# Ten ring slots for twelve, gathers worked on two at a time, and ten weight chunks kept for both blocks

## What is computed

```python
for i in range(DEPTH):                      # DEPTH = 2
    y = rmsnorm(h, mix_norm_g[i])
    h = h + (mixer_ab(y, ...) if i == 0 else mixer_conformer(y, ...))
    y = rmsnorm(h, ffn_norm_g[i])
    h = h + peer(y, peer_w_q[i], peer_sub_keys[i], peer_u[i], peer_v[i])
return rmsnorm(h, final_norm_g)[:, 16:272]

def mixer_conformer(y, ...):
    a, g = split(y @ w_pw1 + b_pw1)         # w_pw1: 1024 x 2048
    z = causal_depthwise_conv(a * sigmoid(g), conv_w) + conv_b   # 31 taps
    return silu(layernorm(z)) @ w_pw2 + b_pw2

def peer(y, w_q, sub_keys, u, v):
    q = (y @ w_q).reshape(T, 8, 2, 128)
    # top 16 of 128 keys for each half, then the top 16 of the 256 sums
    gate = softmax(top_val)
    act = gate * gelu(sum_d(u[expert] * y))
    return sum over heads and experts of act * v[expert]
```

## Time and profile before

| | us |
|---|---|
| median of 3 runs (1606.29 to 1609.34) | 1606.82 |
| the profiled execution | 1606.77 |
| its span, first to last instruction | 1605.0 |

### The profile page before, as it was taken

How to read it: one execution, slowest core, us unless ns; L and a number is a source line. 1 busy time by engine, 2 the same in 40 slices (tenths; PEclk the granted TensorE clock), 3 DMA queues, 4 the chain that set the end, 5 groups by cost and what they waited for, 6 DMA issues and landing times.

```text
span 1605.0 us, 19986 instructions
## 1 busy us (share of the span) xinstructions
PE 1046.8 (65%) x6936; PEld 711.0 (44%) x6936; DVE 1111.9 (69%) x3119; ACT 461.3 (29%) x953; POOL 500.8 (31%) x541
## 2 busy tenths in 40 slices
PE   8997876757734577778574477877576444544454
PEld 8995642525511266656362155665263111211111
DVE  3436878676457776997756777987765777777764
ACT  4111553111111345742111335743222111111110
POOL 0003333333223333332322323332332333333330
PEclk9998877867955699888796589877788555555666
DMA  9979999999999999999999999999999999999994
GB/s 369 408 259 402 374 420 421 417 421 420 416 420 420 421 378 415 420 415 394 422 416 420 421 411 403 417 405 374 420 418 419 421 422 421 421 421 423 420 420 190
DMA packets 105300, 646.70 MB, mean 403 GB/s; under 512 B 11632, under 2 KB 15728, under 8 KB 37616
## 3 DMA queue, kind: packets, MB, share of 16 engines
q0 software_dynamic: 76032, 553.68, 83.5%
q1 hardware_dynamic: 25536, 89.66, 14.2%
q10 hardware_dynamic: 3632, 2.08, 0.4%
HBM read 644.33 MB, written 1.05 MB: 402 GB/s over the span
## 4 chain that ended last, share of the span: by engine, by line
DMA 40%; PE 28%; DVE 15%; POOL 5%; issue 5%; ACT 4%; DVEq 2%; POOLq 0%; ACTq 0%
DMA ring<-in_uv_dram,expert 36%; PE ps L691 14%; DVE ring L1221 7%; PE ps L868 7%; POOL ring L406 5%; DMA wring<-in_wall_dram 5%; PE ps L881 2%; DVE side L1276 2%; PE ps L698 1%; PE ps L909 1%; ACT side L590 1%; PE ps L856 1%; ACT yg L471 1%; ACT osb L651 1%; ACT L475 0%
## 5 line engine op out<-in xcount | busy, mean ns | idle before, releaser
L1221 DVE CUSTOM_DVE_ANT_0 ring<-ring,ps 128x1024 f32<-128x1024 f32 x528 | 634.8, 1217 | 314.9 <-DMA ring<-in_uv_dram,expert 261.2
L406 POOL DMA_INDIRECT ring<-in_uv_dram,expert x528 | 498.7, 945 | 1068.8 <-PE ps L868 808.2
L868 PE MATMUL ps<-ring,mix 128*32 128x512 f32 x2112 | 369.3, 834 | 327.3 <-DVE mix L1237 327.3
L868 PEld LDWEIGHTS ps<-ring,mix 128*32 128x32 f32 x2112 | 67.8, 135 | 531.7 <-DVE mix L1237 391.0
L665 ACT ACTIVATE gel<-dots 128x4 f32<-128x4 f32 x132 | 27.1, 205 | 761.7 <-DVE dots L1221 761.4
L691 PE MATMUL ps<-yT,wring 128*128 128x128 f32 (+1 forms) x1184 | 159.6, 294 | 48.2 <-DMA wring<-in_wall_dram 27.6
L691 PEld LDWEIGHTS ps<-yT,wring 128*128 128x128 f32 x1184 | 150.7, 202 | 63.6 <-DMA wring<-in_wall_dram 34.2
L881 PE MATMUL ps<-sel,osb 128*128 128x16 f32 x528 | 84.1, 304 | 70.6 <-ACT osb L651 70.6
L881 PEld LDWEIGHTS ps<-sel,osb 128*128 128x128 f32 x528 | 80.7, 241 | 108.9 <-ACT osb L651 108.9
L590 ACT ACTIVATE side<-ident,params 128x128 f32<-128x128 f32 x310 | 96.3, 389 | 15.6 <-PE ps L909 14.8
L856 PE MATMUL ps<-ident,yg 128*128 128x128 f32 x264 | 48.0, 342 | 58.0 <-DVE dots L1221 58.0
(11 more groups left out here) (211 smaller groups left out, 1135.5 us busy)
## 6 DMA issues: line engine op xcount, KB each, us to landing
wring<-in_wall_dram SPq DMA_DIRECT2D x102, 512.0 KB, 11.8
ring<-in_wall_dram SPq DMA_DIRECT2D x44, 512.0 KB, 14.5
kept<-in_wall_dram SPq DMA_DIRECT2D x24, 512.0 KB, 17.0
ring<-in_uv_dram,expert POOLq DMA_INDIRECT x528, 16.1
out_dram<-fo ACTq DMA_DIRECT2D x16, 64.0 KB, 6.7
hT<-in_xT_dram ACTq DMA_DIRECT2D x1, 576.0 KB, 15.9
hT<-in_xT_dram SPq DMA_DIRECT2D x2, 256.0 KB, 3.2
params<-in_smalls_dram ACTq DMA_DIRECT2D x1, 380.0 KB, 17.7
```

Source lines behind the costliest of these rows:

```text
L406: pool.indirect_dma_start(out=ring[:, i % R, :], out_offset=None, in_=uv, in_offset=bass.IndirectOffsetOnAxis(ap=expert[:, n % 2, k:k + 1] ...
L868: mm = pe.matmul(po[32 * j:32 * j + 32, half, :], mix[:, k, :], ring[:, slot, D + 512 * half:D + 512 * (half + 1)], start=(q == 0), stop=( ...
L1221: nc.vector.tensor_tensor_reduce(out=row, in0=row, in1=yrep, scale=1.0, scalar=0.0, op0=ALU.mult, op1=ALU.add, accum_out=dots[:, k:k + 1]) ...
```

## The change

R goes from 12 to 10 and KEEP from 6 to 10; both take 16 KB a partition from or to the same memory. `RB` = 12 chunks instead of 16 lie in `ring` at first, and gathers from the tenth on wait for `s_vm`. Four more chunks of the first projection are kept for both windows, so `STREAM` has 166 entries for 170. Each quad is worked as two pairs e = 2q and 2q + 1: two Gelus of two columns, two calls of `weights` (the first stands behind the quad's second dot and its side work, the second where the quad's stood), and two calls of `values` (both behind the slice of the quad; the last pair of a group stands where the last quad stood, in the next group, while the pair before it stays in its own).

```diff
--- before.py
+++ after.py
@@ -18,8 +18,8 @@
 EPS = 1e-6
 LOW = -3.0e38
 NB = 4
-KEEP = 6
-R = 12
+KEEP = 10
+R = 10
 NDIAG = 20
 
 IN_ORDER = [0, 4, 1, 5, 2, 6, 3, 7, 8, 9, 10, 11, 16, 20, 17, 21, 18, 22, 19, 23, 12, 13, 14, 15]
@@ -123,13 +123,14 @@
 
 
     FREE = 4
-    EARLY = LOADED[JOB["inB", 15 + KEEP]] + 1
+    RB = 2 * (R - FREE)
+    EARLY = LOADED[JOB["inB", RB + KEEP - 1]] + 1
     HELD = [LOADED[JOB["pw10", k]] for k in range(KEEP)]
-    BUFFER = [(i - EARLY) % (NB + 16 + KEEP) for i in range(EARLY)]
+    BUFFER = [(i - EARLY) % (NB + RB + KEEP) for i in range(EARLY)]
     for i in range(EARLY, len(STREAM)):
-        BUFFER.append(NB + 16 + HELD.index(i) if i in HELD else (i - EARLY - sum(j < i for j in HELD)) % NB)
+        BUFFER.append(NB + RB + HELD.index(i) if i in HELD else (i - EARLY - sum(j < i for j in HELD)) % NB)
     BEFORE = [[j for j in range(i) if BUFFER[j] == BUFFER[i]] for i in range(len(STREAM))]
-    assert all(BUFFER[LOADED[JOB["inB", k]]] == NB + k for k in range(16 + KEEP))
+    assert all(BUFFER[LOADED[JOB["inB", k]]] == NB + k for k in range(RB + KEEP))
 
     ctx = ExitStack()
     with ctx:
@@ -252,8 +253,8 @@
             b = BUFFER[i]
             if b < NB:
                 return wring[:, b, :, :]
-            if b >= NB + 16:
-                return kept[:, b - NB - 16, :, :]
+            if b >= NB + RB:
+                return kept[:, b - NB - RB, :, :]
             return flat[:, (4 + b) * D:(5 + b) * D].rearrange("p (c n) -> p c n", n=P)
 
 
@@ -275,7 +276,7 @@
 
         s_x = [sem("s_x0"), sem("s_x1"), sem("s_x2")]
         s_par = sem("s_par")
-        s_w = [sem(f"s_w{b}") for b in range(NB + 16 + KEEP)]
+        s_w = [sem(f"s_w{b}") for b in range(NB + RB + KEEP)]
         s_par2 = sem("s_par2")
         s_const = sem("s_const")
         s_pad = sem("s_pad")
@@ -661,8 +662,9 @@
                 if n:
                     evacuate(n - 1)
                 for q in range(4):
-                    act.wait_ge(s_dot, TOPK * n + 4 * q + 4)
-                    act.activation(gel[:, 4 * q:4 * q + 4], dots[:, 4 * q:4 * q + 4], ACT.Gelu).then_inc(s_gel, 1)
+                    for e in (2 * q, 2 * q + 1):
+                        act.wait_ge(s_dot, TOPK * n + 2 * e + 2)
+                        act.activation(gel[:, 2 * e:2 * e + 2], dots[:, 2 * e:2 * e + 2], ACT.Gelu).then_inc(s_gel, 1)
                     front(4 * n + q)
                     side(n, q)
                     if q == 1 and n > G0:
@@ -856,13 +858,14 @@
                     last = pe.transpose(yrep[:, c * P:(c + 1) * P], yg[:, c, :, :].rearrange("p h t -> p (h t)"), ident[:, :])
                 last.then_inc(s_yr, 1)
 
-            def values(n, q):
-
-                pe.wait_ge(s_m, 4 * n + q + 1)
-                if q == 0 and n:
+            def values(n, e):
+
+                q = e // 2
+                pe.wait_ge(s_m, 8 * n + e + 1)
+                if e == 0 and n:
                     pe.wait_ge(s_oe, n)
                 for half in range(2):
-                    for j in range(4):
+                    for j in (2 * (e % 2), 2 * (e % 2) + 1):
                         k = 4 * q + j
                         slot = (n * TOPK + k) % R
                         mm = pe.matmul(po[32 * j:32 * j + 32, half, :], mix[:, k, :],
@@ -943,18 +946,19 @@
                 if n:
                     rows(n)
                 if n:
-                    values(n - 1, 3)
+                    values(n - 1, 7)
                     back(n - 1)
                 for q in range(4):
                     front(4 * n + q)
                     side(n, q)
+                    values(n, 2 * q)
                     if q < 3:
-                        values(n, q)
+                        values(n, 2 * q + 1)
                     if q == 2 and n + 2 < N:
                         scores(n + 2)
                     if q == 2 and n > G0:
                         final_sums(n - 1)
-            values(N - 1, 3)
+            values(N - 1, 7)
             back(N - 1)
             final_sums(N - 1)
 
@@ -1221,21 +1225,21 @@
                 nc.vector.tensor_tensor_reduce(out=row, in0=row, in1=yrep, scale=1.0, scalar=0.0, op0=ALU.mult,
                                                op1=ALU.add, accum_out=dots[:, k:k + 1]).then_inc(s_dot, 1)
 
-            def weights(n, q):
-
-                ks = slice(4 * q, 4 * q + 4)
-                if q == 0:
+            def weights(n, e):
+
+                ks = slice(2 * e, 2 * e + 2)
+                if e == 0:
                     dve.wait_ge(s_exp, n + 1)
                     nc.vector.reciprocal(grec[:, :], gsum[:, n % 2:n % 2 + 1])
                     dve.drain()
-                dve.wait_ge(s_gel, 4 * n + q + 1)
+                dve.wait_ge(s_gel, 8 * n + e + 1)
                 nc.vector.scalar_tensor_tensor(out=coef[:, ks], in0=gel[:, ks], scalar=grec[:, :],
                                                in1=gexp[:, n % 2, ks], op0=ALU.mult, op1=ALU.mult)
                 if n:
-                    dve.wait_ge(s_vm, TOPK * (n - 1) + 4 * q + 4)
+                    dve.wait_ge(s_vm, TOPK * (n - 1) + 2 * e + 2)
                 dve.drain()
-                nc.vector.tensor_tensor(mix[:, ks, 0:GT], coef[:, ks].unsqueeze(2).to_broadcast([P, 4, GT]),
-                                        sel[:, :].unsqueeze(1).to_broadcast([P, 4, GT]), ALU.mult).then_inc(s_m, 1)
+                nc.vector.tensor_tensor(mix[:, ks, 0:GT], coef[:, ks].unsqueeze(2).to_broadcast([P, 2, GT]),
+                                        sel[:, :].unsqueeze(1).to_broadcast([P, 2, GT]), ALU.mult).then_inc(s_m, 1)
 
             def add_back(n):
                 dve.wait_ge(s_ot, n + 1)
@@ -1358,6 +1362,8 @@
                             side(n, q - 1, i)
                         elif n:
                             side(n - 1, 3, i)
+                        if i == 1:
+                            weights(n, 2 * q)
 
                     if q == 0 and n + 1 < N:
                         route_pairs(n + 1)
@@ -1367,7 +1373,7 @@
                         finish(n - 2)
                     if q == 3 and n + 2 < N:
                         route_best(n + 2)
-                    weights(n, q)
+                    weights(n, 2 * q + 1)
                     if q == 0 and n:
                         add_back(n - 1)
                     if q == 2 and n > G0:
```

## The result

The changed kernel takes 1697.09 us (median of 4 runs, 1691.88 to 1699.83), 1.0553 of the time before (95% interval 1.0533 to 1.0574): 90 us slower, where 28 were forecast. Its profiled execution took 1691.88 us, with a span of 1690.1 us.

What follows compares the result with a forecast made beforehand. Bound by DMA: bytes at 421 GB/s plus DMA's idle time. Terms -5 - 5 + 12 + 12 + 4 + 9 + 2 - 1 = +28 on 1606.8 gave 1635 us, slower; range 1600 to 1662, the forecast case's own 1616 to 1656.

Steps and rivals of the forecast that it cites:

- The bound and the stretches: Whole kernel: DMA-bound at 421 GB/s; in three computing stretches more computing is more time, elsewhere it costs nothing.
- The new wait on VectorE: After a quad's second dot: 1.8 us stalls for the Gelu in half the 16 convolution quads; perhaps 0.3 us elsewhere, +4.
- the dearest: Rival "the slots decide": seven dips pay 5 us each, the Gelu wait costs 20, 1669 us; chance 0.13.
- The doubled instructions: Weight steps on VectorE and ScalarE: 0.3 to 0.44 us more a quad, within the convolution's +12.
- Values in pairs: TensorE: a pair takes a quad's 1.92 us, exposed in 8 quads of the first projections, +12.
- The slots: Ten gather slots for twelve: three computing stretches lose 3 us each, +9, bounds 0 and 35.
- a stretch pays once: Computing stretches: dips share their loss; only DMA's lead at the end, two slots less, is lost once.
- the rival in which each dip pays: Rival "the slots decide": each of seven dips pays 5 us, +35 rather than +9, 1669 us; chance 0.13.
- 8 outstanding both times: Gathers in steady stretches: 12 - 4 or 10 - 2 outstanding, 20 us of transfer, so nothing changes there.
- The bytes and the waits for weights: Layer 1's first projection: four chunks fewer loaded, -5; TensorE's shorter waits for chunks in two windows, -5.
- The first gathers: Kernel start: gather 10 waits for the first pair's values, seven us later; 0 to 5, taken as +2.
- the tail: Kernel end: the last values may run at the higher clock; 0 to -1.7, taken as -1.

Runs made afterwards that it cites:

- e13: Kernel before (twelve slots, quads) with VectorE's weight step in two halves, one right behind the other, no new wait: 1626.68 us, 1.0061.
- e17: Kernel before with ScalarE's Gelu in halves and VectorE waiting for the first half behind each quad's second dot, nothing else moved: 1669.37 us, 1.0328.
- e2: Changed kernel with the old sizes, twelve slots and six kept chunks, all three engines in pairs: 1680.73 us, 1.0450.
- e5: e2 with VectorE's weight step of the even pair behind the quad's fourth dot instead of its second: 1634.89 us, 1.0155.
- e4: Kernel before's twelve slots and six kept chunks, pairs on ScalarE and VectorE alone with the new wait, values by quads: 1678.05 us, 1.0432.
- e7: Kernel before with only TensorE's values as two pairs, both after the quad's weight step, the seventh pair beside the eighth: 1608.12 us, 0.9991.
- e1: Kernel before with the change's sizes alone, ten slots and ten kept chunks, quads as before: 1651.6 us, 1.0264.
- e10: e1 with only six chunks kept for both windows, the four other places unused after layer 0: 1.0220.
- e16: Changed kernel with only six chunks kept for both windows, the four other places unused after layer 0: 1.0543.
- e14: Kernel before with two of layer 1's chunks kept for both windows instead of six: 1621.66 us, 1.0039.
- e6: Changed kernel with VectorE's weight step of the even pair behind the quad's fourth dot instead of its second: 1671.0 us, 1.0374.

## Why the prediction was wrong

**The bound and the stretches** were right. The lag arises in the three stretches where the dots hardly wait for gathers; the DMA-bound stretches hid nearly everything, and 82 us of waits for the Gelu in them don't show in the lag. That more computing is more time there "one for one" was too strong: the instructions of e13, 26 us by that rule, cost 10, and the 91 us of waits of e17 cost 53.

**The new wait on VectorE** is the step that failed, by its size. The prediction put stalls of 1.8 us into half of the convolution's quads, 14 us in all, and 4 us elsewhere; with the doubled instructions that made the terms 12 + 4 us, bounds 0 to 36 + 10. The wait by itself measured 53 us (e17), and e2 against e5, where it is moved, 47. The changed kernel has 66 us of these waits in its computing stretches. 12 of them stand in the convolution's quads, where the prediction put 14, though 9 of these at groups' heads and not behind diagonals alone; 54 stand elsewhere, where it put 4. I asked what stands ahead of the Gelu on ScalarE in one kind of quad and not in all: at a group's head it is up to three table loads, the gates, a row copy and a copy that itself waits for TensorE, and at group 0 and in the first projection the copies at TensorE's pace. The discount was not at fault: I took 12 us for 21 of stalls and instructions, a factor of 0.6, and e17 has nearly the same. What was missed is the waits outside the convolution. No rival had it either; the dearest priced the wait at 20 us.

**The doubled instructions** (7 us for the convolution's quads, nothing elsewhere) measured 10 us over all stretches (e13), interval 6 to 14. That was about right.

**Values in pairs** (+12) were wrong. A pair alone does take what a quad takes: 8 records in 1.91 us here, 16 in 1.92 us before. By the Trainium skill ("TensorE: Matmul & The Clock Gate", Part 3: Packing small matmuls) matmuls on different tiles run at once, and a pack lasts about as long as one matmul. The trace agrees with that. Yet in six of the eight quads of the first projections, where the term was put, the pairs come back to back, and there the 16 records take 1.94 to 2.04 us together (timeline of TensorE after, two pairs at once and one alone):

```profile
629.72 1.94 PE L871 MATMUL ps<-ring,mix 128*32 128x512 f32 x16
...
1680.12 1.91 PE L871 MATMUL ps<-ring,mix 128*32 128x512 f32 x8 [1.30 <-DVE mix L1241]
```

The second pair writes to the two tiles that the first leaves free, and its matmuls add 0.03 us where each pair by itself takes 1.91. TensorE's busy time for the values rose from 369 to 557 us because elsewhere the pairs come apart. A third of that, 63 us, falls into the computing stretches; these are the rows of the second one, the kernel before (565 to 770 us) and after (windows view of the line of the values):

```profile
565.00:770.00 205.00, 33.39 (x272) 7.20 (x272) 0.88 0.99 405
...
593.00:828.00 235.00, 52.27 (x280) 10.91 (x272) 0.85 0.86 343
```

Even so it cost little: from e4 to e2, which adds just this, it is 3 us, within the noise, and e7, with all pairs back to back, shows no difference.

**The slots** (+9, bounds 0 to 35) measured 16 us in the change (1.0553 to 1.0450, the kept chunks included), 35 once the wait is gone and 42 with quads. My argument that a stretch pays once was wrong in e1, where the lag grows in almost every group: the rival in which each dip pays was nearer. In the change it was partly covered: VectorE, held up by the Gelu, came later to its gathers, and its dots waited for them 10.3 us in the second stretch, where e1's waited 26.1. That this is why the price fell from 42 to 16 us is argued, not shown. And the count "8 outstanding both times" did not save it: pairs at ten slots cost 27 to 35 us over pairs at twelve.

**The bytes and the waits for weights** (-5 and -5) came to nothing at ten slots (e10, e16). The prediction had said that the bytes are worth 0 if they fall into a computing stretch; they do. The ring in front of a window holds four chunks whichever they are (12 loads from 840 to 985 us in both runs), so what is saved is not what was prefetched at 840 us but what was reloaded in the middle of the projection. And ten chunks have to be loaded ahead of the first window for six before, which costs some 5 us in group 7; the prediction had no term for that. The waits did shrink, from 29.2 to 22.5 us. At twelve slots four chunks (2 to 5) are worth 6 us (e14), so the nothing of e10 and e16 holds for ten slots alone.

**The first gathers** (+2) and **the tail** (-1) were small and right in sign. Group 0 takes 1.1 us longer in e1, which has the ten slots alone. From the last group's head to the end it is 50.4 us after and 53.9 before. In this trace the last pair ran at the higher clock, 1.91 us for 3.64, and so did the 16 matmuls behind it, 1.96 us for 3.60: together 3.4 of the 3.5 us.

So of 90 us: the wait some 50 (53 in e17, 47 from e2 to e5), the doubled instructions 10, another 10 of the pairs unexplained, the slots with the kept chunks 16. The parts are not strictly additive, as e6 shows, where the slots cost 35.

## What to carry to other kernels

When a step is split so that an in-order engine waits in the middle of its work, list what stands ahead of the awaited instruction on the other engine at every place of the schedule, the heads of loops first, and price the wait by the worst of these in the stretches where the waiting engine sets the pace. A transfer saved is worth only what DMA lacks in the stretch in which it would have been issued, and keeping data resident can move other loads into a stretch where they cost (group 7). Wait as late as the data allows: the same pairs with the step two dots later were 47 us faster.

## What was not expected of the hardware

Matmuls on column tiles from two separate calls, with a semaphore wait between them that had already been met, overlap as if they were one: 16 records in 1.94 us against 1.91 us for 8. And TensorE's granted clock was higher where the values took longer: in the long last stretch it went from 0.65, with TensorE busy 214 of 411 us (1140 to 1551 us before), to 0.83, with 267 of 420 us (1220 to 1640 us after). DMA bounds that stretch, and the gain that shows in the time is the 3.5 us of the tail.
